# Head norms in 32-column strips of TensorE, the sampled attention ordered by head pair, and two units of the projection moved behind the output projection

## What is computed

```python
def hgrn2_mixer(q_in, f_in, i_in, g_in, lb, g_norm, s0):
    ...
    o, s_final = gated_linear_recurrence(q, k, v, logf, s0, chunk)
    o = rms_norm(o, g_norm.reshape(N_REC_HEADS, REC_DV)) * jax.nn.silu(heads(g_in))
...
def sample_attention(q, k, v, ck, cv, rel_bias):
    k_all = jnp.concatenate([ck.astype(k.dtype), k], axis=1)   # 256 cached keys and 8 new ones
    v_all = jnp.concatenate([cv.astype(v.dtype), v], axis=1)
    res = [dilated_gather_attention(q, k_all, v_all, rel_bias, w, d) for w, d in DILATED_PATTERNS]
    return mix_patterns([r[0] for r in res], [r[1] for r in res])
...
    attn = rms_norm(attn, g_attn_out.reshape(N_ATTN_HEADS, ATTN_HEAD_DIM))...
    mixed = jnp.einsum('btc,cd->btd', jnp.concatenate([rec_out, attn], axis=-1), w_out)
    x = x + rms_norm(mixed, g_mix_post)
    h = rms_norm(x, g_mlp_pre)
```

## Time and profile before

| | |
|---|---|
| median of three runs | 1661.73 us |
| profiled execution | 1659.98 us, its span 1658.1 us |
| TensorE matmuls, busy | 1600.8 us, 12176 records |
| VectorE, ScalarE, GpSimd busy | 966.7, 832.4, 197.2 us |
| granted clock of TensorE, mean | 0.989 of full |
| DMA | 247.82 MB, 149 GB/s on the mean |

### The profile page before, as it was taken

One profiled execution on the slowest core, in us unless ns is written; L12 is line 12 of the kernel. 1 busy time (PEld: TensorE's weight loads), 2 busy tenths in 40 slices (PEclk: granted clock), 3 DMA queues, 4 the chain that ended last, 5 costly groups with the idle time before them and its releaser, 6 DMA issues.

```text
span 1658.1 us, 30046 instructions
## 1 busy us (share of the span) xinstructions
PE 1600.8 (97%) x12176; PEld 1524.4 (92%) x12176; DVE 966.7 (58%) x1597; ACT 832.4 (50%) x1482; POOL 197.2 (12%) x225
## 2 busy tenths in 40 slices
PE   5999999989999999999999999999999999999996
PEld 5998779988999999999899987899889999999995
DVE  6753646594456655335987445467744575553475
ACT  6426443447464755334664363434664566551552
POOL 3220103120000100000213100142100010000011
PEclk9999999999999999999999999999999999999998
DMA  5544553334355555334454454343534545552443
GB/s 197 190 143 158 199 194 109 121 132 141 106 162 153 165 180 185 120 111 146 152 153 123 152 208 174 127 137 94 172 105 138 165 151 170 187 181 90 128 153 108
DMA packets 83188, 247.82 MB, mean 149 GB/s; under 512 B 8771, under 2 KB 26435, under 8 KB 82924
## 3 DMA queue, kind: packets, MB, share of 16 engines
q1 hardware_dynamic: 83052, 245.90, 46.7%
HBM read 234.05 MB, written 14.44 MB: 150 GB/s over the span
## 4 chain that ended last, share of the span: by engine, by line
PE 87%; DVE 8%; ACT 2%; DMA 1%; issue 1%; SPq 0%; POOLq 0%; POOL 0%; DVEq 0%; ACTq 0%
PE ps L955 66%; PE ps L952 6%; PE ps L1019 3%; DVE w_rest L1275 2%; PE ps L1155 1%; PE ps L1168 1%; PE ps L1183 1%; PE ps L1198 1%; DVE reg L1313 1%; DVE square_sum L1288 1%; DMA kc<-kcT 1%; DVE norm_every L1298 1%; PE ps L1221 1%; PE ps L1108 1%; PE ps L1253 1%
## 5 line engine op out<-in xcount | busy, mean ns | idle before, releaser
L955 PE MATMUL ps<-h_high,w_rest 128*128 128x320 f32 (+1 forms) x1920 | 580.7, 302 | 7.2 <-DVE h_rest L1333 6.2
L955 PE MATMUL ps<-h_high,w_high 128*128 128x320 f32 (+1 forms) x1920 | 569.3, 297 | 0.0
L955 PE MATMUL ps<-h_rest,w_high 128*128 128x320 f32 (+1 forms) x1920 | 569.3, 297 | 0.0
L702 ACT ACTIVATE w_high<-w_raw 128x1024 fp32r<-128x1024 f32 x384 | 402.1, 1052 | 233.3 <-PE ps L955 233.0
L1275 DVE TENSOR_TENSOR w_rest<-w_raw,w_high 128x1024 fp32r<-128x1024 f32 x380 | 480.8, 1269 | 64.6 <-ACT w_high L702 64.3
L955 PEld LDWEIGHTS ps<-h_high,w_rest 128*128 128x128 f32 x1920 | 365.2, 190 | 24.5 <-issue 20.1
L955 PEld LDWEIGHTS ps<-h_rest,w_high 128*128 128x128 f32 x1920 | 365.5, 190 | 0.4
L955 PEld LDWEIGHTS ps<-h_high,w_high 128*128 128x128 f32 x1920 | 365.3, 190 | 0.0
L955 PE MATMUL ps<-u_high,w_rest 128*128 128x320 f32 (+1 forms) x1024 | 305.3, 298 | 3.9 <-DVE u_rest L1375 3.2
L955 PE MATMUL ps<-u_high,w_high 128*128 128x320 f32 (+1 forms) x1024 | 303.1, 296 | 0.0
L955 PE MATMUL ps<-u_rest,w_high 128*128 128x320 f32 (+1 forms) x1024 | 303.1, 296 | 0.0
(11 more groups left out here) (176 smaller groups left out, 1763.2 us busy)
## 6 DMA issues: line engine op xcount, KB each, us to landing
w_raw<-w SPq DMA_DIRECT2D x384, 512.0 KB, 3.5
kc<-kcT SPq DMA_DIRECT2D x16, 512.0 KB, 6.8
vc<-vc SPq DMA_DIRECT2D x16, 512.0 KB, 6.6
s_in<-s SPq DMA_DIRECT2D x8, 512.0 KB, 5.7
ss<-s_in SPq DMA_DIRECT2D x8, 512.0 KB, 5.7
bias<-rel_scratch SPq DMA_DIRECT2D x8, 512.0 KB, 4.4
rel_scratch<-rel_row SPq DMA_DIRECT2D x1, 2560.0 KB, 12.8
bias<-rel_scratch SPq DMA_DIRECT2D x8, 256.0 KB, 5.3
```

Source lines behind the costliest of these rows:

```text
L702: A.activation(whi[:, v % RING], raw[:, v % RING], ACT.Copy).then_inc(S["w_hi"], 1)
L955: last = pe.matmul(ps[:, bank, 0:n], wt[:, slot, c, :], xt[:, c, :], **flags)
```

## The change

The norms of the heads keep the head sums on the partitions and the tokens in the columns. `r_sum` makes four products, one for each head, in four strips of 32 columns with all tokens of the half moving (320 or 256); `a_sum` does so for each head pair with a 0/1 matrix of 32 columns, and adds the denominators' part with eight more products, two for each strip. Root and reciprocal run on 128 rows by 320 (256) columns, in one shared tile `rn`, so that the two norms wait for each other's spread. The spreads are one product for each head or pair, from the rows 32a (one row) or 32j (two rows) of `rn`.

The rows of the sampled attention are ordered by head pair, then sequence, head of the pair and token. `s_sc` makes eight products of 264 keys in four 32-column strips; `s_pv` makes 24 products of 128 columns in such strips, 16 with the cached values and 8 with the own ones; the mask works on 256 columns, and `s_sel` makes two products of 32 columns. `q_big` copies 4 pieces in place of 8.

In the order, two outputs of IB (the last two of QA) move behind OA, `r_sum` and `r_spr` of half 0 come one output earlier (7, 8, 9), the two first level steps of half 1 both hang on IB 10, and behind OA `upd`, `norm_sum`, `post` and `pre` hang on 18 to 25 in place of 21 to 27.

```diff
-IB_CUT = 20
+IB_CUT = 18
-    cut = 18
+    cut = 16
-    put("IB", 8, "r_sum", 0)
-    put("IB", 9, "r_spr", 0, 0)
-    put("IB", 10, "r_spr", 0, 1)
+    put("IB", 7, "r_sum", 0)
+    put("IB", 8, "r_spr", 0, 0)
+    put("IB", 9, "r_spr", 0, 1)
-            i = 11 + 2 * lv + g
+            i = 10 + max(0, 2 * lv + g - 1)
-    put("IB", 21, "upd", 1)
-    put("IB", 21, "norm_sum", 1, 0)
+    put("IB", 18, "upd", 1)
+    put("IB", 18, "norm_sum", 1, 0)
-        put("IB", 21 + p // 2, "post", 1, 0, p)
+        put("IB", 18 + (p + 1) // 2, "post", 1, 0, p)
-    put("IB", 24, "norm_sum", 2, 0)
+    put("IB", 22, "norm_sum", 2, 0)
-        put("IB", 25 + p // 2, "pre", 2, 0, p)
+        put("IB", 23 + (p + 1) // 2, "pre", 2, 0, p)
...
 ScalarE
+                if l or h:
+                    act.wait_ge(S["a_spr"], 8 * l + 4 * h)
+                A.activation(rn[:, 0:n], ps[:, 2, 0:n], ACT.Sqrt, bias=eps[:], scale=1.0 / P).then_inc(S["r_root"], 1)
...
 TensorE, r_sum and r_spr
-                for t, (t0, rows) in enumerate(TILES[h]):
-                    for a in range(HR):
-                        o0 = 4 * t + a
-                        last = pe.matmul(ps[0:rows, 2, o0:o0 + 1], o_sq[h][:, a, t0:t0 + rows], ones[:, 0:1],
-                                         start=True, stop=True)
+                for a in range(HR):
+                    last = pe.matmul(ps[32 * a:32 * a + 32, 2, 0:WIDE[h]], ones[:, 0:32], o_sq[h][:, a, :], start=True, stop=True)
...
+                    pe.matmul(ps[:, 3 + i, 0:WIDE[h]], ones[32 * a:32 * a + 1, :], rn[32 * a:32 * a + 1, 0:WIDE[h]],
+                              start=True, stop=True).then_inc(S["r_spr"], 1)
...
 TensorE, s_sc
-                for j in range(HP):
-                    for s in range(2):
-                        last = pe.matmul(ps[64 * s:64 * s + 64, 5, 0:PAST + TB], q[:, j, 64 * s:64 * s + 64], kc[s][:, j, :],
-                                         start=(j == 0), stop=(j == HP - 1))
+                for s in range(2):
+                    for j in range(HP):
+                        last = pe.matmul(ps[32 * j:32 * j + 32, 5, 0:PAST + TB], q[:, s, j, :], kc[s][:, j, :],
+                                         start=(s == 0), stop=(s == 1))
...
 TensorE, s_pv
+                for s in range(2):
+                    for k2 in range(2):
+                        for j in range(HP):
+                            q0 = k2 * P + 32 * j
+                            pe.matmul(ps[32 * j:32 * j + 32, 7, P * s:P * s + P], pts[:, q0:q0 + 32],
+                                      vcs[p % 2][s][:, k2, P * j:P * j + P], start=(k2 == 0), stop=False)
+                    for j in range(HP):
+                        q0 = 2 * P + 32 * j
+                        last = pe.matmul(ps[32 * j:32 * j + 32, 7, P * s:P * s + P], pts[0:TS, q0:q0 + 32],
+                                         va[0][0:TS, 2, P * j:P * j + P], start=False, stop=True)
...
 TensorE, a_sum
+                for j in range(HP):
+                    pe.matmul(ps[32 * j:32 * j + 32, 2, 0:WIDE[h]], head_sum, a_sq[h][:, j, :], start=True, stop=False,
+                              skip_group_check=True)
+                for c in range(2):
                     for j in range(HP):
+                        c0 = HA * c + 2 * j
+                        last = pe.matmul(ps[32 * j:32 * j + 2, 2, pro(h, c)], den2[:, c0:c0 + 2], ident,
+                                         start=False, stop=(c == 1), skip_group_check=True)
...
 VectorE, r_sum and a_sum
+                V.reciprocal(rn[:, 0:n], rn[:, 0:n]).then_inc(S["r_inv"], 1)
+                V.reciprocal(rn[:, 0:n], rn[:, 0:n]).then_inc(S["a_inv"], 1)
```

More of the change, by code:

```diff
@@ L265, in constants @@
     eye = np.eye(P, dtype=np.float32)
-    half = np.kron(np.eye(2), np.ones((DH, DH))).astype(np.float32)
     row = np.arange(P)
+    sums = (row[:, None] // DH == np.arange(32)[None] % 2)
+    spread = (row[:, None] % 32 == np.arange(P)[None] // DH)
     seq_of_tok = (row % TS // TB)[:, None] == np.arange(NB)[None]
-    head_of_row = ((row % 64) // TB)[:, None] == np.arange(HA)[None]
-    tok_of_row = (row // 64 * TB + row % TB)[:, None] == np.arange(2 * TB)[None]
-    cst = np.concatenate([eye, half, seq_of_tok, head_of_row, tok_of_row], 1).astype(np.float32)
+    pair, seq, head, tok = row // 32, row // 16 % 2, row // TB % 2, row % TB
+    head_of_row = head[:, None] == np.arange(2)[None]
+    col = np.arange(HP * TB)[None]
+    tok_of_row = (pair[:, None] == col // TB) & (tok[:, None] == col % TB)
+    tok_of_row = np.concatenate([tok_of_row & (seq == i)[:, None] for i in range(2)], 1)
+    cst = np.concatenate([eye, spread, seq_of_tok, sums, tok_of_row, head_of_row], 1).astype(np.float32)
     s, r = np.arange(P)[:, None], np.arange(P // 2)[None]
@@ L354, in build @@
     den = place("den", [P, 2 * HA])
-    den2 = place("den2", [P, 3 * HA])
-    root = place("root", [P, 3 * HA])
-    inv = place("inv", [P, 3 * HA])
-    r_root = place("r_root", [P, 3 * HR])
-    r_inv = place("r_inv", [P, 3 * HR])
+    den2 = place("den2", [P, 2 * HA])
+    rn = place("head_norm", [P, WIDE[0]])
     assert at[0] <= 229344, at[0]
     ident = cst[:, 0:P]
-    half_ones = cst[:, P:2 * P]
+    head_spread = cst[:, P:2 * P]
     seq_mask = cst[:, 256:264]
-    head_mask = cst[:, 264:272]
-    tok_sel = cst[:, 272:288]
+    head_sum = cst[:, 264:296]
+    tok_sel = [cst[:, 296 + 32 * i:328 + 32 * i] for i in range(2)]
+    head_mask = cst[:, 360:362]
     def part(h, first):
@@ L493, in rel_tab @@
                 b, h = n // HA, n % HA
-                rows = slice(64 * b + TB * h, 64 * b + TB * h + TB)
+                rows = slice(32 * (h // 2) + 16 * b + TB * (h % 2), 32 * (h // 2) + 16 * b + TB * (h % 2) + TB)
                 if n == 0:
@@ L1134, in r_spr @@
                 pe.wait_ge(S["r_inv"], 2 * l + h + 1)
+                take(3, 4)
                 for i in range(2):
                     a = 2 * g + i
-                    take(3 + i)
-                    for t, (t0, rows) in enumerate(TILES[h]):
-                        last = pe.matmul(ps[:, 3 + i, t0:t0 + rows],
-                                         r_inv[0:rows, 4 * t + a:4 * t + a + 1].broadcast_to([rows, P]),
-                                         ident[0:rows, 0:rows], start=True, stop=True)
-                    last.then_inc(S["r_spr"], 1)
+                    pe.matmul(ps[:, 3 + i, 0:WIDE[h]], ones[32 * a:32 * a + 1, :], rn[32 * a:32 * a + 1, 0:WIDE[h]],
+                              start=True, stop=True).then_inc(S["r_spr"], 1)
                     held[3 + i] = (S["r_mul"], 8 * l + 4 * h + a + 1)
@@ L1217, in s_pv @@
                 take(7)
-                for k2 in range(2):
-                    for s in range(2):
-                        q0 = k2 * P + 64 * s
-                        pe.matmul(ps[64 * s:64 * s + 64, 7, :], pts[:, q0:q0 + 64], vcs[p % 2][s][:, k2, :],
-                                  start=(k2 == 0), stop=False)
-                pe.matmul(ps[:, 7, :], pts[0:TS, 256:384], va[0][0:TS, 2, :], start=False, stop=True).then_inc(S["spv_done"], 1)
+                for s in range(2):
[8 more added lines that the diff above has]
+                                         va[0][0:TS, 2, P * j:P * j + P], start=False, stop=True)
+                last.then_inc(S["spv_done"], 1)
                 held[7] = (S["mo_set"], n + 1)
@@ L1229, in s_sel @@
                 take(7)
-                for j in range(HP):
-                    last = pe.matmul(ps[:, 7, 16 * j:16 * j + 16], mo[p % 2][:, j * P:j * P + P], tok_sel, start=True, stop=True)
+                for s in range(2):
+                    dst = ps[:, 7, 0:TS].rearrange("p (j s t) -> p j s t", j=HP, s=2)[:, :, s, :]
+                    last = pe.matmul(dst, mo[p % 2][:, s, :], tok_sel[s].rearrange("p (j t) -> p j t", j=HP), start=True, stop=True)
                 last.then_inc(S["sel_done"], 1)
```

76 lines of the change are left out of this document (32 added, 44 removed).

## The result

The changed kernel takes 1637.23 us as the median of four runs (1630.39 to 1638.05), the kernel before 1661.84 beside it: a ratio of 0.9836 with the interval [0.98, 0.9872]. The forecast was 1627.0 with the range 1617 to 1642. The time lies in the range, 10 us above the value; of 34.7 us expected, 24.6 came.

A forecast was written before the change was run, and what follows sets the result against it. TensorE, busy 97% of the span, was taken to bound the kernel. Savings of 39.0 us, less 2 x (0.75 + 2.1) for waits, plus 2 x 0.7 for order, gave 34.7 us: 1627 us, range 1617 to 1642.

The forecast's parts named there:

- the price of the steps: Shorter small steps on TensorE, sampled attention and norms: saves 19.5 us a layer, 39.0 in all.
- the record floor: Rival: records no closer than 0.054 us, hitting steps of many short records such as values; 1636 us, 15 in 100.
- the larger waits: Rival: both later key loads bind and the sum of squares waits 3 us more; 1637 us, 17 in 100.
- Four strips beside each other: Assumption for the small TensorE steps: four column strips run beside each other as two do; no row showed four.
- the strips in twos: Rival: strips run only two at a time in scores, values and sums, giving back 23 us; 1650 us, 8 in 100.
- the strips one after the other: Rival: four strips don't run beside each other at all, 70 us back; 1697 us, 4 in 100.
- Spreads beside each other: Norm spreads: two products from different 32-row groups and banks overlap, 0.7 (0.6) us; saves 5.6 us a layer.
- Copies of the probabilities: Last pair's transposed probabilities, copied late by ScalarE, make TensorE wait at line 1221: +2.1 us a layer.
- The wait for the last pair's keys: TensorE's wait for the last pair's cached keys grows from 0.47 to 1.2 us: +0.75 a layer.
- Behind the output projection: Wait for the pre-MLP sum of squares, asked for at 22 instead of 24, grows from 5.1 to 6 to 7 us.
- The order was worth 1.4 us: Reordered projection: longer sum-of-squares wait against more cover for the right half, net gain 0.7 us a layer.
- the half clock: Rival: the sampled stage's half-clock stretch moves away and the norm order hides part of a wait; 1618 us, 6 in 100.

The follow-up runs named there:

- e1: Changed kernel with the new steps but the old order of the projection, against the kernel before: 1632.75 us, ratio 0.9814.
- e8: Changed kernel with both products of each spread reading the same 32-row group instead of two: 1637.01 us in one run.
- e2: Old steps in the new order, against the kernel before: 1668.42 us, ratio 1.0013.
- e4: Changed kernel with the recurrent norm of half 0 back at outputs 8, 9 and 10: 1633.5 us, ratio 0.9813.
- e9: Changed kernel, norm back, nine unread products before the pre-MLP sum-of-squares wait, one before the first score step, three before the last: 1628.47 us, ratio 0.9776.

## Why the prediction was right, and where it was off

The time lies in the stated range, and the main term, the price of the steps, holds. But 1637 lies outside the 1621 to 1634 that the prediction gives as its forecast's own range, and it is the figure of two of its rivals, the record floor (1636) and the larger waits (1637). Neither is what happened: the floor is refuted by the rows below, and waits took 2.9 us more than forecast where that rival has 9. That the range held is in part luck: it was made wide for these two, and what used up most of the distance to its slow end was the clock, which has no term in the sum.

- **The price of a step**: right nearly everywhere. 0.15 us for a change of split and 0.107 us for 128 columns of the longest strip gave 1.03, 1.9, 0.4, 0.7 and 0.7 for scores, values, selection, recurrent sum and spread, and 1.1 for attention's sum; the rows have 1.03, 1.85, 0.47, 0.68, 0.74 and 1.11. The work fell by 37.6 us where the sum had 39.0; e1, with the same steps in the old order, has 36.5. Most of the rest is the selection and the spreads, 0.04 to 0.07 us each.
- **Four strips beside each other**, the one assumption: right. Line 1220's 16 records take 0.574 us, 0.036 each with the entry, and its starts lie 0.025 us apart on the mean; four of line 1196 begin within 0.02 us. The figure of 62 ns that the Trainium skill ("TensorE: Matmul & The Clock Gate", Part 1) gives for a matmul that the sequencer's microcode decodes, by which the value step would have been 3.0 us as an estimate, doesn't hold here either. So the record floor of 0.054 us, the strips in twos and the strips one after the other are all out, as is a weight load that waits for the pass before it.
- **Spreads beside each other**: right, and e8 shows what it hangs on.
- **Copies of the probabilities**: +2.1 forecast, 2.3 measured in each layer. (The prediction's terms 0.7, 0.4, 0.3 and 2.87 add up to 4.3 us, not the 4.4 that it writes; with 4.3 its own sum comes to 2.3.) The wait for the last pair's keys was to be 1.2 us and is 0.3 in layer 0, because TensorE comes to it later: 1.3 and 0.7 us stand ahead of the first pair instead. The total for keys rose by 1.5, which is what I had, at another place.
- **Behind the output projection**: 6 to 7 us in each layer forecast in one wait; the rows have 1.7 us for a K output's bank and 4.9 for the sum of squares, 6.6 together. Both hang on one chain of VectorE: post's steps and weight rests. ScalarE empties the K output's bank only after it has had squares to make, for which it waited 3.09 us on VectorE, and that ends TensorE's wait of 1.72 us:

```profile
323.74 0.83 ACT L712 ACTIVATE squares<-x 128x320 f32<-128x320 f32 x2 [3.09 <-DVE square_sum L1293]
324.48 0.36 ACT L783 ACTIVATE key<-ps 128x256 f32<-128x256 f32 x1
...
324.98 0.36 PE L959 MATMUL ps<-h_high,w_rest 128*128 128x256 f32 x1 [1.72 <-ACT key L783]
```

The gain on the other side was 1.62 to 0.39 us ahead of the transposes. I had counted about half a microsecond more in gains there and a net of +0.7 a layer; it is about -0.3. Together with 0.7 us that line 1235 now waits, this is most of the term on waits that was too good, 7.2 us in place of 4.3. The rival on waits also has VectorE busy 8 us more in each layer; the page has 8.2 us more in the two layers together.
- **The order was worth 1.4 us** in the forecast as a net gain behind the output projection. e2 and e1 show nothing: -0.8 and +1.1 us at the same clock. And the earlier norm costs more than its wait was priced at: with it back where it was, e4 is 3 us faster. The price of +2.1 a layer was right, but it was not set against leaving the norm where it stood.
- **The clock**: the step that failed. The forecast carried the half clock only as a rival that would bring more gain, and its base, the profiled execution at 0.989, was taken for the kernel's time. It was one of its better draws: 41 runs have their median at 1665.8, and at their mean clock the forecast would have been 1631, and the changed kernel's runs come to 1634.9 at that clock. Of the ten us between forecast and result some 6 are this (4 the base, 2 the lower clock of the result's runs, of which the new order may have a part), 3 the waits, 1 the steps.

## What to carry to other kernels

Steps with few rows out or few rows in are worth packing in four strips of 32 (priced at the longest strip's passes and one entry of 0.15 us; strips of rows must lie in different 32-row groups), but a step ahead of a wait is worth less than its length. A change of the order should be timed apart from the rest, since here it brought nothing. Before a difference of some microseconds is explained, set the mean granted clock of each run beside its time: here 0.001 of it was 1.4 us, and draws of one kernel lay 13 us apart. But don't correct it away where the edit itself may move the clock: then set the distributions of the clock side by side, and see in two or more traces of one kernel which stretches at half clock recur.

## What the hardware showed

Four records in four strips begin within 0.02 us of each other and last together 0.43 us where one lasts 0.41; over a whole step the starts are 0.025 us apart on the mean (16 records of 128 columns take 0.574 us with the entry). It makes no difference in which order the strips stand in the list (1.03 and 1.05 us). Two products with one row of weights each run beside each other from different 32-row groups (0.74 us for both) and one after the other from the same group (1.27 us). TensorE fell to 1.2 GHz in stretches of 3.4 or 6.8 us. Six of seven came at the same places in two executions of the changed kernel, others in only one of them. One came with TensorE busy 7.90 of 7.90 us ahead of it (203.90 in e9). Nine executions in which TensorE was idle for 4.9 to 5.1 us ahead of the sum of squares all fell to 1.2 GHz in that idle time, in both layers; the four in which products left 0.8 to 1.3 us of it idle did not.
